# Head loop of a gated-DeltaNet block: the first TensorE level of a triangular inverse by 32x32 corners alone, turned on VectorE

## The chip, the cores and the metric

The kernel runs on one core of one Trainium2 chip. The metric is the device time of one execution in microseconds; the median of several executions is given. All engines of the core (TensorE, VectorE, ScalarE, GpSimd, and SyncE that mostly issues DMAs) have instruction streams of their own and meet at semaphores that the kernel sets and waits for.

## The reference

One decoder block over 1024 tokens of width 1024, in fp32: a mixer (gated DeltaNet beside a short convolution, merged by gates), then a mixture of 32 experts. The part that the change touches is the chunked gated delta rule, with 8 heads of width 128:

```python
    decay = jnp.where(causal, jnp.exp(jnp.where(causal, diff, 0.0)), 0.0)
    k_beta = k * beta
    a = jnp.where(strict, jnp.einsum('bhnik,bhnjk->bhnij', k_beta, k) * decay, 0.0)
    eye = jnp.eye(CHUNK, dtype=a.dtype)
    t_inv = lax.linalg.triangular_solve(eye + a, jnp.broadcast_to(eye, a.shape),
                                        left_side=True, lower=True, unit_diagonal=True)
    u = jnp.einsum('bhnij,bhnjv->bhniv', t_inv, v * beta)
    w = jnp.einsum('bhnij,bhnjk->bhnik', t_inv, k_beta * jnp.exp(g)[..., None])
    intra = jnp.einsum('bhnik,bhnjk->bhnij', q, k) * decay
```

A scan over the chunks follows, which carries a 128x128 state from chunk to chunk. The kernel uses chunks of 128 tokens, so a head has 8 tiles (`TT = 8`), each with a unit lower triangular 128x128 matrix to invert.

## The kernel before

The kernel is one program in stages: adaLN and norm, projections of the short convolution and the gates, the loop over 8 heads, the merge with the output projection, the routing, and the experts. The large projections are fp32 products made of three products of rounded parts (`w_hi`, `w_lo` against `h_hi`, `h_lo`): ScalarE rounds a weight tile to `w_hi` (`split_w_hi`, L698), VectorE subtracts it for `w_lo` (`split_w_lo`, L703), TensorE multiplies (`project`, L769).

In the head loop TensorE's queue is written out by hand, and projections of the same and the next head are put between the small products of the delta rule so that TensorE has work while other engines answer. Part `n` of the third projection of a head (`third(n)`, 2 to 3 of the 8 k-tiles, 6 or 9 products) is such work, and so are the 3-product pieces (`filler`) in the recurrence.

The inverse of each 128x128 triangle grows in levels. VectorE inverts the 16x16 diagonal blocks (`sub_inverse`), results go through DRAM to other lanes (`inverse_rows` on SyncE), GpSimd spreads them over X (L874), VectorE makes the cross blocks that join them to 32x32 (`pair_inverse`), and four DMAs put those into X (L1112, with `base_moved`). X then holds the inverses of the four 32x32 diagonal blocks of each of the 8 tiles. VectorE's transpose (`turn_inverse`, L2103) turns 32x32 blocks, which is a full turn of this block diagonal matrix, and gives Y, the transpose of X.

Two levels on TensorE follow, in `head_pe` and `head_dve`, each over halves `a` of four tiles:

- Level 0 joins 32x32 blocks to 64x64. TensorE multiplies the whole 128x128 `kk_decay` by X (L2905). VectorE scales by -beta and masks with `level_mask` (L2202), which keeps the corner blocks: LX. TensorE multiplies by Y (L2938), VectorE adds the result to X (L2222).
- Level 1 joins 64x64 to 128x128. TensorE multiplies (L2908) and turns X as a whole with eight transposes to PSUM (L2913), from which VectorE copies the new blocks into Y (L2209). VectorE scales (L2197, no mask), TensorE multiplies by Y (L2943), VectorE adds to Y (L2226). X is not needed any more.

Between a level's first and second product TensorE has `third(1)` and `third(2)`, and in front of level 1's second product also eight transposes of v (L2921). VectorE has a weight part (`split_w_lo`) in each level and `q_dec` in the second. Then TensorE makes w from Y (L2950) and the recurrence over the 8 tiles begins (L2980 to L2994), in which the fillers of projection 3 run. Behind it come projection 4, the norm of o, and the keys of the next head. In the last head there is no `third`, and the fillers multiply by `so_hi` and `so_lo`, which DMAs bring back from DRAM (L1151, issued when the head's third projection is done).

The masks are made by GpSimd at the start (L799 to L807). `NL` is the number of levels, `HP` is 64.

Of the kernel before, what the change touches and what calls it, by code (L numbers as in the profile page):

```python
# [5 lines left out]
ALU = mybir.AluOpType  # L6
# [6 lines left out]
P = 128  # L13
# [36 lines left out]
def decoder_block(nc, x, c, w_ada, b_ada, norm1_g, w_in, conv_qkv_w, a_log, dt_bias, onorm_g, w_proj_a,  # L50
# [4 lines left out]
    TT = T // P  # L55
# [17 lines left out]
    LEVELS = [32, 64]  # L73
# [51 lines left out]
    level_mask = at("level_mask", [P, len(LEVELS), P])  # L125
# [314 lines left out]
    with ctx:  # L440
# [332 lines left out]
        def blocks_of(tile, n, odd):  # L773

            return tile.rearrange("p (m s r) -> p m s r", s=2, r=LEVELS[n])[:, :, odd, :]

        def half_dst(bank, t, n):

            return ps[:, bank, (t % 4) * P // 2:(t % 4 + 1) * P // 2].rearrange("p (m r) -> p m r", r=LEVELS[n])

        N_MASKS = 1 + len(LEVELS)

        @block.gpsimd
        def _(pool):
# [5 lines left out]
            pool.memset(level_mask[:], 0.0).then_inc(pool_step, 1)  # L790
            pool.wait_ge(pool_step, 4)
# [6 lines left out]

            for n, b in enumerate(LEVELS):  # L799
                even = level_mask[:, n].rearrange("p (m s r) -> p m s r", s=2, r=b)[:, :, 0, :]  # L800
                src = ones[:].rearrange("p (m s r) -> p m s r", s=2, r=b)[:, :, 0, :]
                m = P // (2 * b)
                pool.affine_select(out=even, in_=src, compare_op=ALU.is_ge, fill=0.0, base=-b,
                                   pattern=[[-2 * b, m], [0, b]], channel_multiplier=1).then_inc(pool_step, 1)
                pool.wait_ge(pool_step, 5 + n)
                pool.affine_select(out=even, in_=even, compare_op=ALU.is_ge, fill=0.0, base=2 * b - 1,
                                   pattern=[[2 * b, m], [0, b]], channel_multiplier=-1).then_inc(masks_done, 1)  # L807

# [4 lines left out]
            pool.wait_ge(pool_step, 6 + len(LEVELS))  # L813
# [85 lines left out]
            pool.wait_ge(pool_step, 9 + len(LEVELS))  # L899
# [836 lines left out]
        def _(dve):  # L1736
# [443 lines left out]
            def head_dve(h, last):  # L2180
# [10 lines left out]

                for n in range(NL):
                    for a in range(2):
                        dve.wait_ge(lx_mm, 2 * NL * h + 2 * n + a + 1)
                        tiles = slice(4 * a, 4 * a + 4)
                        if n == NL - 1:
                            ins = dve.tensor_tensor(  # L2197
                                LX[HP:, tiles, 0:HP], ps[HP:, 6 + a].rearrange("p (t i) -> p t i", i=P)[:, :, 0:HP],
                                hk[HP:, K_NBETA, tiles, None].to_broadcast([HP, 4, HP]), ALU.mult)
                        else:  # L2200
                            for t in range(4 * a, 4 * a + 4):
                                ins = dve.scalar_tensor_tensor(  # L2202
                                    out=LX[:, t], in0=ps[:, 6 + a, (t % 4) * P:(t % 4 + 1) * P],
                                    scalar=hk[:, K_NBETA, t:t + 1], in1=level_mask[:, n], op0=ALU.mult, op1=ALU.mult)
                        ins.then_inc(lx_done, 1)
                        if n > 0:
                            dve.wait_ge(yl_mm, 2 * NL * h + 2 * (n - 1) + a + 1)
                            y_odd = blocks_of(Y[:, tiles].rearrange("p t i -> p (t i)"), n - 1, 1)
                            dve.tensor_copy(y_odd, blocks_of(ps[:, 2 + a], n - 1, 1)).then_inc(y_upd, 1)  # L2209
                    split_w_lo(dve, *(("merge", 0, n) if last else ("head", h, 3 + n)))  # L2210
                    if n == NL - 1:
                        dve.wait_ge(silu_done, 3 * h + 2)
                        dve.wait_ge(grow_in, 16 * h + 32)
                        dve.tensor_tensor(q_dec[:].rearrange("p t i -> p (t i)"), qk[:, 0],
                                          grow[:].rearrange("p t i -> p (t i)"), ALU.mult).then_inc(q_dec_done, 1)
                    for a in range(2):
                        tiles = slice(4 * a, 4 * a + 4)
                        if n < NL - 1:
                            dve.wait_ge(xl_mm, 2 * (NL - 1) * h + 2 * n + a + 1)
                            x_even = blocks_of(X[:, tiles].rearrange("p t i -> p (t i)"), n, 0)  # L2220
                            change = ps[:, 4 + a, 0:2 * P].rearrange("p (m r) -> p m r", r=LEVELS[n])
                            dve.tensor_tensor(x_even, x_even, change, ALU.add).then_inc(x_upd, 1)  # L2222
                        else:
                            dve.wait_ge(yl_mm, 2 * NL * h + 2 * n + a + 1)
                            y_odd = blocks_of(Y[:, tiles].rearrange("p t i -> p (t i)"), n, 1)[0:HP]
                            dve.tensor_tensor(y_odd, y_odd, ps[0:HP, 2 + a, 0:2 * P]  # L2226
                                              .rearrange("p (m r) -> p m r", r=LEVELS[n]), ALU.add).then_inc(y_upd, 1)
# [1050 lines left out]
```

## Time and profile before

| | |
|---|---|
| median of 3 executions | 1977.56 us (1976.2 to 1979.18) |
| the profiled execution, its span | 1977.9 us |
| TensorE busy | 1908.4 us, 96% |
| VectorE busy | 1473.9 us, 75% |
| ScalarE busy | 982.2 us, 50% |
| GpSimd busy | 314.5 us, 16% |
| HBM | 356.89 MB read, 58.06 MB written |

Times in the profile are from the start of the span. An engine row names the line of the kernel that made the instruction. TensorE appears twice: PE for the products, PEld for the weight loads, which run beside them. An fp32 product appears as two records of each; a product of rounded parts and a transpose as one. The start of a record is measured and its end is modelled, so that neighbouring products overlap in the rows and their pace is the distance of their starts.

### The profile page before, as it was taken

The page shows a single profiled execution, that of the slowest core. Times are in us where ns is not written, and L with a number is a line of the kernel's source. Part 1 is how long each engine was busy: PE and PEld are TensorE (multiplying, and loading weights), DVE is VectorE, ACT ScalarE, POOL GpSimd, SP SyncE. Part 2 cuts the span into 40 slices and gives each one's busy share as a digit, 9 for nine tenths or more (in the row PEclk, how much of TensorE's full clock was granted, in tenths as well). Part 3 has the DMA queues.
Part 4 walks back from the last instruction along what each step waited for, and adds up shares of the span by engine and source line. Part 5 has one row for each costly group of instructions (what it writes and reads, how often), then busy time and mean ns, then how long its engine had stood idle before and what let it go on. Part 6 is the DMA issues. An engine that isn't in the chain of part 4 may idle for free.

```text
span 1977.9 us, 28478 instructions
## 1 busy us (share of the span) xinstructions
PE 1908.4 (96%) x9519; PEld 1584.6 (80%) x9519; DVE 1473.9 (75%) x1966; ACT 982.2 (50%) x1354; POOL 314.5 (16%) x243
## 2 busy tenths in 40 slices
PE   5999999999999999999999899998999999999996
PEld 5778888778888888888888787876888888888883
DVE  6966676676756858658577455677999999999996
ACT  5343223301453544535535343125888788788863
POOL 0332323001102101021011000001222222222210
PEclk7999999999999999999999999998999999999998
DMA  8133223687132222222232678437999999999966
GB/s 301 32 82 103 68 80 106 213 294 248 40 106 72 70 75 77 80 70 71 84 93 59 206 266 262 140 143 280 372 383 383 382 380 381 386 387 383 400 252 257
DMA packets 225500, 398.93 MB, mean 202 GB/s; under 512 B 50805, under 2 KB 163878, under 8 KB 199974
## 3 DMA queue, kind: packets, MB, share of 16 engines
q1 hardware_dynamic: 205254, 342.28, 49.8%
q10 hardware_dynamic: 10976, 39.15, 5.1%
q0 software_dynamic: 9216, 16.80, 2.2%
q8 instruction: 32, 0.52, 0.1%
q14 instruction: 22, 0.18, 0.0%
HBM read 356.89 MB, written 58.06 MB: 210 GB/s over the span
## 4 chain that ended last, share of the span: by engine, by line
PE 70%; DVE 13%; DMA 6%; ACT 5%; issue 5%; SPq 1%; ACTq 0%; DVEq 0%; POOL 0%; POOLq 0%
PE ps L3152 17%; PE ps L2756 13%; PE ps L769 12%; PE ps L3196 9%; PE ps L3047 4%; PE ps L2786 3%; PE ps L3138 1%; DVE vv L2019 1%; DMA inv_rows<-inv_d 1%; DMA so_lo<-o_lo_d 1%; DMA inv_d<-sub_x 1%; PE ps L2950 1%; PE ps L2980 1%; PE ps L3176 1%; PE ps L2994 1%
## 5 line engine op out<-in xcount | busy, mean ns | idle before, releaser
L637 DVE TENSOR_TENSOR mw_lo<-mw_raw,mw_hi 128x2048 fp32r<-128x2048 f32 x192 | 436.9, 2290 | 44.0 <-ACT mw_hi L632 43.8
L632 ACT ACTIVATE mw_hi<-mw_raw 128x2048 fp32r<-128x2048 f32 x192 | 368.1, 1919 | 116.2 <-PE ps L3152 67.0
L769 PE MATMUL ps<-h_hi,w_lo 128*128 128x512 f32 x704 | 287.9, 409 | 3.0 <-ACT mod_rows L1447 1.3
L769 PE MATMUL ps<-h_hi,w_hi 128*128 128x512 f32 x704 | 275.5, 391 | 0.0
L769 PE MATMUL ps<-h_lo,w_hi 128*128 128x512 f32 x704 | 274.9, 391 | 0.0
L3152 PE MATMUL ps<-mw_hi,xT_lo 128*128 128x512 f32 x512 | 203.9, 398 | 3.1 <-DVE xT_lo L2525 2.3
L3152 PE MATMUL ps<-mw_hi,xT_hi 128*128 128x512 f32 x512 | 201.1, 393 | 0.0
L3152 PE MATMUL ps<-mw_lo,xT_hi 128*128 128x512 f32 x512 | 200.3, 391 | 0.0
L769 PEld LDWEIGHTS ps<-h_hi,w_hi 128*128 128x128 f32 x704 | 132.6, 188 | 28.4
L769 PEld LDWEIGHTS ps<-h_hi,w_lo 128*128 128x128 f32 x704 | 133.0, 189 | 26.6 <-ACT conv_in L1454 1.8
L769 PEld LDWEIGHTS ps<-h_lo,w_hi 128*128 128x128 f32 x704 | 133.2, 189 | 22.3
L909 POOL DMA_INDIRECT xg<-h_d,tok_now x32 | 80.8, 2524 | 292.8 <-DVE tok_now L2515 276.3
L3152 PEld LDWEIGHTS ps<-mw_hi,xT_lo 128*128 128x128 f32 x512 | 96.8, 189 | 23.3 <-DVE xT_lo L2525 2.9
L3152 PEld LDWEIGHTS ps<-mw_hi,xT_hi 128*128 128x128 f32 x512 | 96.7, 189 | 21.0
L3152 PEld LDWEIGHTS ps<-mw_lo,xT_hi 128*128 128x128 f32 x512 | 96.9, 189 | 19.3
L698 ACT ACTIVATE w_hi<-w_raw 128x1024 fp32r<-128x1024 f32 x60 | 62.1, 1050 | 93.3 <-DMA w_raw<-in_w_proj_b_dram 59.6
L874 POOL TENSOR_TENSOR X<-inv_rows,sub_mask 128x128 f32<-128x128 f32 x64 | 49.2, 804 | 335.2 <-DMA inv_rows<-inv_d 335.2
L1856 DVE TENSOR_TENSOR comb<-ps,comb 128x512 f32<-128x512 f32 x98 | 66.4, 689 | 47.0 <-PE ps L2756 43.9
L3196 PE MATMUL ps<-mw_hi,hidT_lo 128*128 128x512 f32 x248 | 99.2, 400 | 0.0
L703 DVE TENSOR_TENSOR w_lo<-w_raw,w_hi 128x1024 fp32r<-128x1024 f32 x60 | 74.1, 1236 | 30.3 <-ACT w_hi L698 29.0
L3196 PE MATMUL ps<-mw_lo,hidT_hi 128*128 128x512 f32 x248 | 96.7, 390 | 0.0
L3196 PE MATMUL ps<-mw_hi,hidT_hi 128*128 128x512 f32 x248 | 96.6, 390 | 0.0
(436 smaller groups left out, 4042.4 us busy)
## 6 DMA issues: line engine op xcount, KB each, us to landing
mw_raw<-in_w_dram SPq DMA_DIRECT2D x192, 1024.0 KB, 8.2
w_raw<-in_w_in_dram SPq DMA_DIRECT2D x44, 512.0 KB, 5.0
ada_h<-in_w_ada_dram SPq DMA_DIRECT2D x32, 512.0 KB, 6.0
pair_w<-in_w_in_dram SPq DMA_DIRECT2D x28, 512.0 KB, 4.8
y_t<-y_d SPq DMA_DIRECT2D x7, 1024.0 KB, 10.1
ada_sc<-in_w_ada_dram SPq DMA_DIRECT2D x4, 1024.0 KB, 8.7
s_d<-sc_acc ACTq DMA_DIRECT2D x8, 512.0 KB, 5.5
gate_b_d<-gate_sig ACTq DMA_DIRECT2D x8, 512.0 KB, 5.0
```

Of the source, the lines that this page charges most:

```text
L632: act.activation(mw_hi[off % NSPLIT][:], mw_raw[off % NRAW][:], ACT.Copy).then_inc(mw_hi_done, 1)
L637: dve.tensor_tensor(mw_lo[off % NSPLIT][:], mw_raw[off % NRAW][:], mw_hi[off % NSPLIT][:], ALU.subtract).then_inc(mw_lo_done, 1)
L698: act.activation(w_hi[:, t["slot"]], w_raw[:, t["slot"]], ACT.Copy).then_inc(w_hi_done, 1)
L703: dve.tensor_tensor(w_lo[:, t["slot"]], w_raw[:, t["slot"]], w_hi[:, t["slot"]], ALU.subtract).then_inc(w_lo_done, 1)
L769: last = pe.matmul(dst, lhs[:, s, k], rhs[:, k, cols], start=(k == 0 and part == 0), stop=(k == KD - 1 and part == 2))
L909: pool.indirect_dma_start(xg[:, s], None, h2_d, bass.IndirectOffsetOnAxis(tok_now[:, s:s + 1], axis=0), bounds_check=T - 1, oob_is_err=Fal ...
L1856: dve.tensor_tensor(out[:], ps[:, bank], other[:], ALU.add).then_inc(combined, 1)
L2756: last = pe.matmul(ps[:, bank], (op_lo, op_hi, op_hi)[part][o][:, k], moving((0, 1, 0)[part], k), start=(k == 0 and part == 0), stop=(k == ...
L2786: last = pe.matmul(ps[:, 2 + 2 * p + half], (w_lo, w_hi, w_hi)[part][:, s, k], (s_hi, s_lo, s_hi)[part][k][:, cols], start=(k == 0 and par ...
L3047: last = pe.matmul(ps[:, 2 * s + half], lhs, rhs[:, k, half * HALF:(half + 1) * HALF], start=(k == 0 and part == 0), stop=(k == KD - 1 and ...
L3152: last = pe.matmul(dst, lhs[:, k0 + k], rhs[:, cols], start=(first and k == 0 and part == 0), stop=(final and k == 3 and part == 2))
L3196: last = pe.matmul(ps[:, bank + half], lhs[:, 2 * part + f], rhs[:, cols], start=(part == 0 and f == 0 and n == 0), stop=(part == 1 and f ...
```

## The change

The constant `LEVELS = [32, 64]` becomes `BLOCK = 32` and `NL = 2`. `level_mask`, its memset and its four selects on GpSimd go; the numbers of the semaphore waits behind them are lowered.

Level 0 no longer runs over whole 128x128 tiles. It runs over the two corners `g` of the block diagonal (rows of block 2g+1, columns of block 2g) for all eight tiles: 32x32 products into 32 partitions of one PSUM bank per corner, with the corner for t = 0 written with 64 rows (`both_blocks`). VectorE scales one corner of all tiles in one operation, without a mask. The product of the corner with Y gives the corner of X, which VectorE copies instead of adding, and VectorE's transpose turns it into Y. The whole transposes of X on TensorE and the copies from them go. Level 1's first product runs without them and waits for the first corner of X only; the second corner is waited for behind `third(2)`, and Y's corners and level 1's LX in front of the last transpose of v. Level 1's second product uses the lower 64 rows alone, and its result is copied to Y instead of added.

```diff
@@ VectorE, head_dve
-                for n in range(NL):
-                    for a in range(2):
-                        dve.wait_ge(lx_mm, 2 * NL * h + 2 * n + a + 1)
...
-                split_w_lo(dve, *(("merge", 0, n) if last else ("head", h, 3 + n)))
...
+                for g in range(2):
+                    dve.wait_ge(lx_mm, 2 * NL * h + g + 1)
+                    dve.tensor_tensor(LX[odd_block(g), :, even_block(g)],
+                                      corner(6, g).rearrange("p (t i) -> p t i", i=BLOCK),
+                                      hk[odd_block(g), K_NBETA, :, None].to_broadcast([BLOCK, TT, BLOCK]),
+                                      ALU.mult).then_inc(lx_done, 1)
+                split_w_lo(dve, *(("merge", 0, 0) if last else ("head", h, 3)))
+                for g in range(2):
+                    dve.wait_ge(xl_mm, 2 * h + g + 1)
+                    dve.tensor_copy(X[odd_block(g), :, even_block(g)],
+                                    corner(4, g).rearrange("p (t i) -> p t i", i=BLOCK)).then_inc(x_upd, 1)
+                for g in range(2):
+                    dve.wait_ge(x_upd, 2 * h + g + 1)
+                    dve.transpose(Y[even_block(g), :, odd_block(g)], X[odd_block(g), :, even_block(g)]).then_inc(y_upd, 1)
+
+                for a in range(2):
+                    dve.wait_ge(lx_mm, 2 * NL * h + 2 + a + 1)
+                    tiles = slice(4 * a, 4 * a + 4)
+                    dve.tensor_tensor(
+                        LX[HP:, tiles, 0:HP], ps[HP:, 6 + a].rearrange("p (t i) -> p t i", i=P)[:, :, 0:HP],
+                        hk[HP:, K_NBETA, tiles, None].to_broadcast([HP, 4, HP]), ALU.mult).then_inc(lx_done, 1)
+                split_w_lo(dve, *(("merge", 0, 1) if last else ("head", h, 4)))
+                dve.wait_ge(silu_done, 3 * h + 2)
+                dve.wait_ge(grow_in, 16 * h + 32)
+                dve.tensor_tensor(q_dec[:].rearrange("p t i -> p (t i)"), qk[:, 0],
+                                  grow[:].rearrange("p t i -> p (t i)"), ALU.mult).then_inc(q_dec_done, 1)
+                for a in range(2):
+                    tiles = slice(4 * a, 4 * a + 4)
+                    dve.wait_ge(yl_mm, 2 * h + a + 1)
+                    dve.tensor_copy(Y[0:HP, tiles, HP:], ps[0:HP, 2 + a, 0:2 * P].rearrange("p (t i) -> p t i", i=HP))\
+                       .then_inc(y_upd, 1)
@@ TensorE, head_pe
+                pe.wait_ge(base_moved, moved(h, 240))
+                for g in range(2):
+                    for t in range(TT):
+                        rows = odd_block if t else both_blocks
+                        last_mm = pe.matmul(corner(6, g, t, rows), kk_decay[even_block(g), t, rows(g)],
+                                            X[even_block(g), t, even_block(g)], start=True, stop=True)
+                    last_mm.then_inc(lx_mm, 1)
+                if not last:
+                    third(1)
+                pe.wait_ge(kk_done, 4 * h + 4)
+                pe.wait_ge(k_bg_done, TT * h + TT)
+                pe.wait_ge(k_dec_done, TT * h + TT)
+                for g in range(2):
+                    pe.wait_ge(lx_done, 2 * NL * h + g + 1)
+                    pe.wait_ge(base_step, OPS * h + PAIR_OPS + 2)
+                    for t in range(TT):
+                        rows = odd_block if t else both_blocks
+                        last_mm = pe.matmul(corner(4, g, t, rows), Y[odd_block(g), t, rows(g)],
+                                            LX[odd_block(g), t, even_block(g)], start=True, stop=True)
+                    last_mm.then_inc(xl_mm, 1)
+
+                pe.wait_ge(x_upd, 2 * h + 1)
+                for a in range(2):
+                    for t in range(4 * a, 4 * a + 4):
+                        at_ = (t % 4) * P
+                        last_mm = pe.matmul(ps[HP:, 6 + a, at_:at_ + HP], kk_decay[:, t, HP:], X[:, t, 0:HP],
+                                            start=True, stop=True)
+                    last_mm.then_inc(lx_mm, 1)
+                if not last:
+                    third(2)
+                pe.wait_ge(silu_done, 3 * h + 3)
+                pe.wait_ge(x_upd, 2 * h + 2)
+                for t in range(TT):
+                    if t == TT - 1:
+                        pe.wait_ge(y_upd, 2 * NL * h + 2)
+                        pe.wait_ge(lx_done, 2 * NL * h + 4)
+                    last_mm = pe.transpose(ps[:, 4 + t // 4, (t % 4) * P:(t % 4 + 1) * P],
+                                           vv[:, t * P:(t + 1) * P], ident[:])
+                    if t % 4 == 3:
+                        last_mm.then_inc(vt_mm, 1)
+                for a in range(2):
+                    for t in range(4 * a, 4 * a + 4):
+                        last_mm = pe.matmul(ps[0:HP, 2 + a, (t % 4) * HP:(t % 4 + 1) * HP], LX[HP:, t, 0:HP],
+                                            Y[HP:, t, HP:], start=True, stop=True)
+                    last_mm.then_inc(yl_mm, 1)
```

The helpers are `even_block(g)` (rows 64g to 64g+31), `odd_block(g)` (64g+32 to 64g+63), `both_blocks(g)` (64g to 64g+63) and `corner(bank, g, t, rows)`, which is `ps[rows(g), bank + g, 32t:32t+32]`.

## Rows read from the trace of the kernel before

**Rows 1.** The page: busy shares, granted clock in 40 slices, ending chain by engine.
```profile
PE 1908.4 (96%) x9519; PEld 1584.6 (80%) x9519; DVE 1473.9 (75%) x1966; ACT 982.2 (50%) x1354; POOL 314.5 (16%) x243
...
PEclk7999999999999999999999999998999999999998
...
PE 70%; DVE 13%; DMA 6%; ACT 5%; issue 5%; SPq 1%; ACTq 0%; DVEq 0%; POOL 0%; POOLq 0%
```

**Rows 2.** Busy time by stretch: from:to, length, busy PE PEld DVE ACT POOL, clock.
```profile
613.00:693.00 80.00, 79.66 (x456) 67.78 (x455) 55.75 (x108) 37.07 (x81) 10.46 (x10) 1.00 0.27 77
...
614.83:623.32 8.49, 8.18 (x67) 7.07 (x65) 7.70 (x18) 3.44 (x4) 0.00 (x0) 1.00 0.00 0
```

**Rows 3.** Chain of waits, 600 to 700 us: start, duration, engine and line.
```profile
600.88 2.64 DMA inv_rows<-inv_d
...
617.54 0.92 DVE LX L2202 x4
...
623.56 2.08 PE ps L769 x9
...
627.62 2.05 PE ps L2950 x16
...
648.56 0.71 PE ps L769 x3
...
697.36 1.00 DVE LX L2202 x4
```

**Rows 4.** Timeline of the second head: start, duration, engine, line, operation, tiles, count.
```profile
611.39 1.74 SPq L1112 DMA_DIRECT2D X<-cross_d  x4
...
614.83 1.95 PE L2905 MATMUL ps<-X,kk_decay 128*128 128x128 f32 x16
...
616.25 1.30 DVE L2103 STREAM_TRANSPOSE Y<-X 128x512 f32<-128x512 f32 x2
...
618.44 0.39 PE L769 MATMUL ps<-h_hi,w_hi 128*128 128x512 f32 x1
618.98 1.97 PE L2938 MATMUL ps<-LX,Y 128*128 128x64 f32 x16 [0.15 <-issue]
...
619.50 1.22 DVE L703 TENSOR_TENSOR w_lo<-w_raw,w_hi 128x1024 fp32r<-128x1024 f32 x1
620.63 0.77 DVE L2222 TENSOR_TENSOR X<-X,ps 128x256 f32<-128x256 f32 x2
621.10 0.68 PE L2908 MATMUL ps<-X,kk_decay 128*64 128x64 f32 x8 [0.15 <-DVE X L2222]
621.71 0.66 PE L2913 MATMUL ps<-ident,X 128*128 128x128 f32 x4
...
623.32 0.47 PE L769 MATMUL ps<-h_hi,w_lo 128*128 128x512 f32 x1
...
625.48 1.03 PE L2921 MATMUL ps<-ident,vv 128*128 128x128 f32 x8
```

**Rows 5.** Weight loads by line: durations ns min/median/max, first and last start us.
```profile
L2905 PEld LDWEIGHTS ps<-X,kk_decay x128: 187/192/193, 535.3 to 1099.9; 128*128 128x128 f32 x128
...
L2684 PEld LDWEIGHTS ps<-h_lo,w_gate_parts x16: 107/108/108, 80.0 to 92.3; 128*32 128x32 f32 x16
...
L2692 PEld LDWEIGHTS ps<-fold,gate_rows x16: 181/187/187, 98.5 to 100.2; 32*128 32x128 f32 x16
```

**Rows 6.** The view of tile X: its DMAs from issue to landing.
```profile
DMA to landing us min/median/max: 1.5/1.7/1.9
```

**Rows 7.** Timeline at the start of the span and in the first head.
```profile
9.93 3.51 PE L2660 MATMUL ps<-ident,x_n 128*128 128x128 f32 x16 [9.93 <-DVE x_n L1769]
...
546.49 1.01 PEld L2943 LDWEIGHTS ps<-Y,LX 128*64 128x64 f32 x16 [0.17 <-issue]
```

**Rows 8.** Timeline of the last head: first DMA for so_hi, and TensorE's wait for them.
```profile
1098.50 0.35 SPq L1151 DMA_DIRECT2D so_hi<-o_hi_d  x1
...
1112.25 0.50 PE L769 MATMUL ps<-so_hi,w_lo 128*128 128x512 f32 x1 [1.08 <-DMA so_lo<-o_lo_d]
```

More of the change, by code:

```diff
@@ L72, in decoder_block @@
     PAIR = 2 * SUB
-    LEVELS = [32, 64]
+    BLOCK = 32
+    NL = 2
     NSUB = P // SUB
@@ L124, in decoder_block @@
     later = at("later", [P, P])
-    level_mask = at("level_mask", [P, len(LEVELS), P])
     sub_mask = at("sub_mask", [P, P])
@@ L771, in project, with even_block, odd_block, both_blocks @@
             return last
[L773 to L781, printed above, removed]
+        def even_block(g):
+            return slice(2 * g * BLOCK, (2 * g + 1) * BLOCK)
+        def odd_block(g):
+            return slice((2 * g + 1) * BLOCK, (2 * g + 2) * BLOCK)
+        def both_blocks(g):
+            return slice(2 * g * BLOCK, (2 * g + 2) * BLOCK)
+        def corner(bank, g, t=None, rows=odd_block):
+            cols = slice(0, TT * BLOCK) if t is None else slice(t * BLOCK, (t + 1) * BLOCK)
+            return ps[rows(g), bank + g, cols]
+        N_MASKS = 1
         @block.gpsimd
@@ L789, in _ @@
             pool.memset(eps_col[:], EPS).then_inc(pool_step, 1)
-            pool.memset(level_mask[:], 0.0).then_inc(pool_step, 1)
-            pool.wait_ge(pool_step, 4)
+            pool.wait_ge(pool_step, 3)
             pool.affine_select(out=ident[:], in_=ident[:], compare_op=ALU.not_equal, fill=1.0, base=0,
@@ L797, in _ @@
                                pattern=[[-1, P]], channel_multiplier=1).then_inc(masks_done, 1)
[L799 to L807, printed above, removed]
             pool.affine_select(out=sub_mask[:].rearrange("p (m r) -> p m r", r=SUB), in_=ones[:].rearrange(
@@ L812, in _ @@
             pool.memset(sub_eye[:], 0.0).then_inc(pool_step, 1)
-            pool.wait_ge(pool_step, 6 + len(LEVELS))
+            pool.wait_ge(pool_step, 5)
             pool.affine_select(out=sub_mask[:].rearrange("p (m r) -> p m r", r=SUB), in_=sub_mask[:].rearrange(
@@ L898, in _ @@
             pool.memset(xg[:], 0.0).then_inc(pool_step, 1)
-            pool.wait_ge(pool_step, 9 + len(LEVELS))
+            pool.wait_ge(pool_step, 8)
             for n in range(2):
@@ L2190, in head_dve @@
                 turn_inverse(h)
-                for n in range(NL):
-                    for a in range(2):
-                        dve.wait_ge(lx_mm, 2 * NL * h + 2 * n + a + 1)
[L2195 to L2209, printed above, removed]
-                    split_w_lo(dve, *(("merge", 0, n) if last else ("head", h, 3 + n)))
[L2211 to L2227, printed above, removed]
@@ L2270, in head_dve @@
                 dve.tensor_tensor(o_lo[:], o_raw[:], o_hi[:], ALU.subtract).then_inc(o_hi_done, 1)
-            NL = len(LEVELS)
             with dve.Fori(0, H - 1) as h:
@@ L2303, in _ @@
             dve.wait_ge(params_in, 16 * 10)
-            dve.wait_ge(pool_step, 8 + len(LEVELS))
+            dve.wait_ge(pool_step, 7)
             steps = [0]
@@ L2821, in _ @@
             pe.wait_ge(gb_sig, past(2 * KD))
-            NL = len(LEVELS)
             o_squares = LX[:].rearrange("p t i -> p (t i)")
```

48 lines of the change are left out of this document (removed).

## The prediction

> **What bounds the kernel now.** I read the page first. TensorE is busy for 96% of the span at a granted clock that stays at its upper level (2.4 GHz) almost everywhere, and 70% of the chain that ended last is TensorE's [rows 1]. The change touches the inverse in the loop over the eight heads (its first products start between 535 and 1100 us [rows 5]) and a few masks built at the very start, so the next view is the busy time by stretch. A steady head takes 80.0 us, and TensorE is busy for 79.66 of them; the first level of the inverse alone, from its first product to the end of its part of the second, takes 8.49 us [rows 2]. So in this loop an engine-microsecond of TensorE is a microsecond of the kernel, unless something else takes over.
>
> The chain of waits shows how close that something is. It does not stay on TensorE: from the end of the recurrence (648.56) it goes over ScalarE's evacuation and VectorE to the small inverses, their DMAs (600.88 is that place one head earlier), VectorE's pair products, its value convolution, the turn of X and the LX products (617.54, and 697.36 one head on), and only behind those back to TensorE [rows 3]. The two LX rows are 79.82 us apart. TensorE's own queue and this VectorE/DMA chain are therefore nearly equally long; both run through the stretch from 617.5 to 627.6 that the change rewrites, so a saving there shortens both. That is the reason to count it in full, head after head.
>
> In the timeline of that stretch [rows 4] the reader is to see three things. First, the 16 records of L2905 (8 products; each fp32 product is two records) start 0.112 us apart ((1.95 - 0.275)/15), and so do those of L2938 although they stream only 64 columns: they are paced by their 128 weight columns. Second, TensorE waits twice for VectorE: L2938 could start at 618.67 (618.44 + 0.23) and starts at 618.98; L2908 starts at 621.10, right behind the first X addition (620.63 + 0.42), and with the change of shape told next it could at 620.94. Together about 0.45 us. Third, a change of tile shape costs (L2908 works on 64 columns, the transposes L2913 on 128). L2908's last record starts at 621.10 + 0.68 - 0.22 = 621.56, the first transpose behind it at 621.71, 0.15 later and not 0.06; the four transposes then need (0.66 - 0.27)/3 = 0.129 and not 0.109 each, the pace of the eight transposes of v ((1.03 - 0.27)/7). Together 0.15 us a change.
>
> **What is removed, per head.** TensorE: 16 records of L2905 at 0.112 = 1.79 us; 16 of L2938 at 0.112 = 1.79; 8 transposes of X (L2913) at 0.109 = 0.87; and the four changes of shape that L2908 and L2913 make in turn, 0.60. Sum 5.05. VectorE: eight LX products, two X additions (0.77 us) and two Y copies.
>
> **What is added, per head.** TensorE: 2 x 8 corner products for LX and 2 x 8 for X, 64 records, with 32 weight columns, 32 moving columns and 32 rows (64 weight columns for t = 0). Call one record's spacing s. Changes of shape: into the corners, t = 0 to t = 1, corner 0 to corner 1, t = 0 to t = 1 again, and out, five for LX and five for X, and one from L2908 back to the projection: 11 x 0.15 = 1.65. Net on TensorE: 5.05 - 1.65 = 3.40 us less, 64 s more.
>
> No row has a record with 32 weight columns and few moving ones, so s is bounded. From above by the 64-column record: the 16 weight loads of L2943 are (1.01 - 0.14)/15 = 0.058 apart [rows 7]. From below by the line through 128 columns (0.112) and 64 (0.058), which gives 0.032 at 32 (an estimate; the single load shortens on such a line too, 192 ns at 128 columns and 108 at 32 [rows 5]). Thirty-two rows alone change nothing: L2692 has them, and its 16 loads run from 98.5 to 100.2, again 0.112 apart [rows 5]. I take s = 0.040, nearer to the line, since the measured loads shorten with the columns all the way, but above it, since a fixed cost per record would show first at the smallest size. Then TensorE's own work falls by 3.40 - 2.56 = 0.84 us a head (1.35 at 0.032; -0.31, longer, at 0.058).
>
> **The stretch played through for head 1, with s = 0.040.** TensorE starts at 614.83 as before; LX corners take 1.28 + 0.60, to 616.71; the nine projection products (2.04 at their pace of 0.23, as in the x9 of [rows 3], and one change) end at 618.90. VectorE still ends its turn of X at 617.55 and makes two LX corners (256 elements a lane as in L2222, 0.42 each) by 618.4, the weight part L703 by 619.6. So TensorE has no wait, does the X corners to 620.78 and is ready for L2908 at 620.93. The first X copy needs the first corner's products (619.8, and 0.2 for their end, the length of a product in L2908) and is there at 620.5. L2908 (16 x 0.058) ends at 621.86, and the projection starts at 622.0 where it started at 623.32: 1.3 us earlier. Behind it VectorE has the second copy (621.4), two transposes of 256 elements (0.42 each, to 622.25), two LX products for level 2, L703 and q_dec (1.22 each, for the same 1024 elements a lane): done at 625.6. TensorE reaches L2943 at 625.14, its first half is out at 625.8, the Y copy follows, and L2950 starts at 626.3 for 627.62. The gain is 1.3 us a head: 0.84 of work and 0.45 of waits. The bounds of s give 1.7 to 1.8 and 0.05 to 0.15.
>
> **Other edits, and what covers them.** TensorE's transposes of v now wait in front of the last one for Y's transposes and for level 2's LX (623.1 here); that one is due at about 624.9, and behind it only L2943 is queued, which needs both anyway. The wait for the second X copy (621.4) stands behind the projection's third part and is 2 us early. ScalarE's copies of v follow the earlier transposes and were idle before them. X must have landed when the corners start: the last of four DMAs is issued by 613.13 and lands 1.7 us later, 614.8 for a start at 614.83 [rows 4, 6]. There is no room in front of the stretch, but that landing is in the chain behind the recurrence and moves with it. The masks: GpSimd drops one memset and four selects at the head of the span, while TensorE's first product starts at 9.93 and had waited for VectorE's x_n [rows 7]: nothing.
>
> **The sum.** In the last head nothing is gained: behind L2980 TensorE waits for the DMAs of so_hi and so_lo until 1112.25, and those are issued from 1098.50, as soon as the projection in front of the corners is done [rows 8]; a shorter inverse makes that wait longer. Seven heads remain: 7 x 1.3 = 9.1 us. The profiled execution has a span of 1977.9 us, 0.3 above the median of the runs shown, 1977.56, so the sum can be set against either: 1977.6 - 9.1 = 1968.5.
>
> **Rivals.**
> 1. *A floor per record.* If a record costs 0.058 however small it is, 64 records and the changes of shape eat what the removed ones gave: -0.31 of work against 0.45 of waits, 0.1 us a head, and 1977 in all. For it: twice the columns take 0.112 and not 0.116, so a record has a fixed part, and no smaller one shows whether that grows into a floor. Chance 0.20.
> 2. *Slower: small tiles don't hide their weight loads.* If in a 32x32 tile the next load can't run under the product in front of it, a record costs its load, 0.108 and more; at the 0.112 of L2905, 64 s is 7.17, TensorE's work grows by 3.77 a head, less 0.45 of waits: 3.3 x 7 = 23, and 2 more in the last head past its DMA wait: 2003. It decides from s = 0.060 on (3.85/64). Against it: in L2943 loads start 0.058 apart, each itself 0.14 long, so that neighbours overlap each other and the products between them [rows 7]. Chance 0.13. The Trainium skill (TensorE: Matmul & The Clock Gate, section on packing small matmuls) says that a weight load overlaps a running matmul only when its row group differs. Here all eight products of a corner have one row group, so by that rule a record would cost a whole load and a whole product, 0.108 and about 0.2, and the kernel some 120 us more; the loads of L2943 overlap on equal rows, which the rule excludes, so I give this form 0.03 of the 0.13.
> 3. *VectorE takes over.* The new chain runs LX corners, L703, X copy, with 0.4 us of room at L2908 and 0.2 at the Y copy. If each of the eight operations on other partitions than the one before starts 0.1 later, L2950 slips by 0.4 to 0.6 and the gain is 0.8 a head: 1972. Chance 0.12. The Trainium skill (VectorE: DVE Perf Modes, section on two Vector instructions with no wait between them) says that an operation whose output starts in another quadrant starts only when all earlier ones have finished; the two X additions here, in one quadrant, overlap by 0.07 (0.77 for 2 x 0.42), and by the rule the new ones would not, 0.4 us on VectorE.
> 4. *The time comes back at the next head.* If X's landing does not move with the recurrence, L2905's place waits for what was saved: 1977. The chain [rows 3] speaks against it. Chance 0.05.
>
> **How the numbers follow.** The forecast, s between 0.032 and 0.05, has 0.50 and ends at 1968.5. Faster by over 0.2% (4 us; about what a measurement of this kernel can tell from no change) are the forecast and rival 3: 0.62. Within 0.2% are rivals 1 and 4: 0.25. Slower is rival 2: 0.13. The range goes down to 1961 (s = 0.032 and the changes from t = 0 to t = 1 free, 0.6 a head more: 7 x 2.35 = 16.5) and up to 1980.5, which takes in rivals 1, 3 and 4 and leaves rival 2 out.
>
> **What would show it.** In the profile of the changed kernel: 64 corner records a head, 0.03 to 0.05 apart, with gaps of 0.15 at the changes; L2908 starting 6.1 us behind the corners' first product, where it is 6.27 now; the projection behind it 7.2 behind, now 8.49; a head period of 78.7 us, now 80.0. Spacings of 0.058 or more, a wait of L2908 for the X copy, or a wait for X's DMA that grows by what was saved would each make the prediction wrong, for rivals 1 or 2, 3 and 4.

## The result and the profile after

| | before | after |
|---|---|---|
| median of the executions | 1977.56 us | 1965.72 us |
| lowest and highest | 1976.2 to 1979.88 | 1964.42 to 1968.72 |
| span of the profiled execution | 1977.9 us | 1962.5 us |

The ratio is 0.9942 (95% interval 0.993 to 0.9954): the change makes the kernel 11.8 us faster, 0.6%. On another chip, beside two of the experiments below (e6_late and e7_order), the same two kernels gave 1978.62 and 1966.66 us, ratio 0.9936 (0.992 to 0.9951). Forecast were 1968.5 us and a range of 1961 to 1980.5.

The page of the changed kernel: busy time, granted clock, and the chain that ended last.

```profile
PE 1897.8 (97%) x9711; PEld 1573.4 (80%) x9711; DVE 1465.7 (75%) x1918; ACT 982.6 (50%) x1354; POOL 313.7 (16%) x238
...
PEclk7999999999999999999999899988999999999998
...
PE 84%; DVE 5%; DMA 5%; ACT 2%; issue 2%; SPq 1%; ACTq 0%; POOL 0%; DVEq 0%; POOLq 0%
```

TensorE has 192 records more and is busy for 10.6 us less. In the chain that ended last its share rose from 70 to 84% and VectorE's fell from 13 to 5% [rows 1]: in the steady heads the detour over VectorE and the DMAs [rows 3] is gone from the chain.

**Where the time went.** Busy time by stretch, from the first product of level 0 in head 0 to that of head 7, in the kernel before and then in the changed one (columns as in [rows 2]):

```profile
535.49:1098.31 562.82, 561.02 (x3198) 477.58 (x3197) 390.62 (x751) 260.78 (x569) 73.16 (x70) 1.00 0.27 76
```
```profile
532.01:1082.56 550.55, 550.25 (x3365) 464.69 (x3365) 383.11 (x709) 260.65 (x569) 73.16 (x70) 1.00 0.27 78
```

Seven head periods shrank by 12.27 us, 1.75 each. The busy columns split this into 10.77 us less work on TensorE and 1.50 us less waiting, of which 0.30 is left; since a product's end is modelled, part of every wait stands in them as busy time, and the starts of the products, used further below, give 2.9 us of waits. From head 7's first product to the end of the span it is 1977.9 - 1098.31 = 879.6 us before and 1962.5 - 1082.56 = 879.9 after. So the gain lies in the seven heads. (That last stretch is from 878.0 to 883.7 us long in the ten profiled executions of this document, so equality to 0.3 us is chance.)

The two spans differ by 15.4 us, 3.5 more than the medians allow. That part lies ahead of head 0 and is TensorE's clock. Busy time by stretch of before, then of after:

```profile
402.00:406.00 4.00, 3.81 (x10) 3.00 (x11) 3.82 (x6) 0.00 (x0) 0.00 (x0) 0.57 1.00 322
...
477.00:481.00 4.00, 4.00 (x12) 3.10 (x11) 3.81 (x6) 0.00 (x0) 0.00 (x0) 0.57 0.98 282
```
```profile
402.00:406.00 4.00, 4.00 (x19) 3.29 (x18) 3.82 (x6) 0.00 (x0) 0.00 (x0) 1.00 1.07 353
...
477.00:481.00 4.00, 4.00 (x19) 3.32 (x18) 3.90 (x9) 0.60 (x1) 0.21 (x1) 1.00 0.38 133
...
1092.00:1096.00 4.00, 4.00 (x20) 3.89 (x18) 0.42 (x1) 0.67 (x2) 0.00 (x0) 0.50 1.03 421
```

Before ran mostly at 1.2 GHz in these two stretches (and in one at 112 us), ten and twelve products where after has nineteen; after had such a stretch in the last head instead. In the first of them TensorE had waited 1.47 us for VectorE's `w_lo` just ahead, in both kernels, and the clock fell in one of the two. The profiled execution of the changed kernel when it ran again had other places once more and the same seven heads (550.56 us). Over the ten profiled executions the start of head 0 goes roughly with the number of such stretches between 100 us and it: 532.01 us with none, 532.69 and 533.25 with one, 533.55 to 535.86 with two, and 535.49 with the three of before. So this part is not put down to the change, and heads are compared from here on, not spans.

**The stretch of head 1**, chain of waits of after, which here is TensorE alone:

```profile
610.15 1.56 PE ps L2886 x32
611.71 2.29 PE ps L769 x9
614.00 1.56 PE ps L2899 x32
615.56 1.07 PE ps L2907 x16
616.63 2.28 PE ps L769 x9
618.91 0.87 PE ps L2918 x8
619.79 1.07 PE ps L2924 x16
620.86 0.04 issue
620.90 2.05 PE ps L2931 x16
...
688.24 1.56 PE ps L2886 x32
```

L2886 and L2899 are the corner products (L2905 and L2938 before), L2907 and L2924 level 1's two products (L2908, L2943), L2918 the transposes of v (L2921), L2931 makes w (L2950). The head period is 688.24 - 610.15 = 78.09 us, for 80.0.

VectorE beside it, timeline of the same head:

```profile
611.42 1.30 DVE L2097 STREAM_TRANSPOSE Y<-X 128x512 f32<-128x512 f32 x2
612.74 0.88 DVE L2188 TENSOR_TENSOR LX<-ps,hk 32x256 f32<-32x256 f32 x2
613.65 1.23 DVE L703 TENSOR_TENSOR w_lo<-w_raw,w_hi 128x1024 fp32r<-128x1024 f32 x1
614.91 0.42 DVE L2195 COPY X<-ps 32x256 f32<-32x256 f32 x1
615.59 0.43 DVE L2195 COPY X<-ps 32x256 f32<-32x256 f32 x1 [0.27 <-PE ps L2899]
```

The first X copy ends at 615.33 and L2907, which needs it, starts at 615.49 in TensorE's timeline. Where it does wait for this copy (e3_few below) it starts 0.05 us behind the copy's end. That is a near tie: 0.1 us of room, where the forecast had 0.4.

### The profile page after: what moved, and what is told of

Same layout as the page of the kernel before. It is cut to its first block, busy times and chain, and to the rows that moved or that the text cites. A ratio compares the mean times of both kernels' runs of the same rounds, so it can differ in the third digit from the quotient of the medians.

```text
span 1962.5 us, 28802 instructions
## 1 busy us (share of the span) xinstructions
PE 1897.8 (97%) x9711; PEld 1573.4 (80%) x9711; DVE 1465.7 (75%) x1918; ACT 982.6 (50%) x1354; POOL 313.7 (16%) x238
## 4 chain that ended last, share of the span: by engine, by line
PE 84%; DVE 5%; DMA 5%; ACT 2%; issue 2%; SPq 1%; ACTq 0%; POOL 0%; DVEq 0%; POOLq 0%
PE ps L769 24%; PE ps L3133 17%; PE ps L2744 13%; PE ps L3177 9%; PE ps L3028 4%; PE ps L2774 3%; PE ps L3119 1%; DMA so_lo<-o_lo_d 1%; PE ps L2961 1%; PE ps L2931 1%; PE ps L2836 1%; PE ps L2865 1%; PE ps L2975 1%; PE ps L3157 1%; PE ps L2964 1%
```

## The experiments

The theories: **P** (the prediction's): both parts of the change shorten TensorE's queue, the removed transposes of X with their changes of shape by about 1.2 us a head, the corners by the rest, each record (one of the two entries that an fp32 product makes in the trace) costing what its weight columns cost. **V**: the queue is already so short that VectorE's chain (LX corners, weight part, X copy) sets the head, so that making TensorE shorter still gives little. **D**: 32x32 tiles in different rows and columns of the array run side by side, so that the order of the corners matters. The first four kernels ran beside 17 executions of the kernel before (median 1979.04 us), the next three beside 11 (1978.62), the last beside 9 (1978.36). The ratio compares a kernel with its own neighbours; medians of different chips are not to be compared with each other. "Seven heads" is always the time from head 0's first product of level 0 to head 7's, in one profiled execution.

| | median us | ratio (95%) | seven heads | TensorE busy in them |
|---|---|---|---|---|
| before | 1977.56 | | 562.82 | 561.02 |
| e1_turn | 1970.11 | 0.9953 (0.994 to 0.9966) | 555.16 | 553.42 |
| changed kernel | 1965.72 | 0.9942 (0.993 to 0.9954) | 550.55 | 550.25 |
| e2_wide | 1970.84 | 0.9951 (0.9938 to 0.9964) | 553.20 | 552.91 |
| e3_few | 1964.24 | 0.9928 (0.9916 to 0.9941) | 549.11 | 545.85 |
| e4_vload | 1975.11 | 0.9981 (0.9972 to 0.999) | 559.46 | 553.77 |
| e6_late | 1963.02 | 0.9921 (0.9908 to 0.9933) | 547.10 | 545.76 |
| e7_order | 1967.34 | 0.994 (0.9927 to 0.9952) | 549.81 | 541.84 |
| e8_best | 1961.98 | 0.992 (0.9906 to 0.9934) | 548.37 | 541.93 |

**The turn alone (e1_turn).** The kernel before, with its whole products and masks, but Y's new blocks come from VectorE's transpose; the PE transposes of X and the Y copies are gone.

```diff
-                        if n > 0:
-                            for t in range(4 * a, 4 * a + 4):
-                                last_mm = pe.transpose(ps[:, 2 + a, (t % 4) * P:(t % 4 + 1) * P], X[:, t], ident[:])
-                            last_mm.then_inc(yl_mm, 1)
...
+                            if a == 1:
+                                dve.wait_ge(x_upd, 2 * h + 2)
+                                for g in range(2):
+                                    even, odd = slice(64 * g, 64 * g + 32), slice(64 * g + 32, 64 * g + 64)
+                                    dve.transpose(Y[even, :, odd], X[odd, :, even]).then_inc(y_upd, 1)
```

> The kernel before with one part of the change alone: VectorE turns the two corners of X into Y, and the eight whole transposes of X on TensorE with their two copies go. The whole-tile products, the masks and the adds stay. Theory P (TensorE's own work in the stretch sets the time): eight transposes at 0.109 us and two of the four changes of tile shape (0.15 each) go, 1.1 to 1.2 us a head in seven heads, 8 us: 1969.5, two thirds of the whole gain. Rival C (the corners bring most of it, because the products shrink from 128 to 32 columns): only the eight transposes' overlap goes, 3 us: 1974.5.

Measured: 562.82 - 555.16 = 7.66 us in seven heads, 1.1 each, as P expected. So about five eighths of the change's 12.27 us come from taking the transposes of X off TensorE, and three eighths (4.61 us, 0.66 a head) from the corners. By the busy columns the corners' share is 3.17 us of TensorE work and 1.44 us of waits.

**64 weight columns in every corner record (e2_wide).**

```diff
-                        rows = odd_block if t else both_blocks
+                        rows = both_blocks
```

> The changed kernel with 64 weight columns in all corner products and not for t = 0 alone: 56 records a head grow from 32 to 64 weight columns, and the four changes of tile shape between t = 0 and t = 1 go. Theory P: a record costs its weight columns (0.032 us at 32, 0.058 at 64), so +1.47 us, less 4 x 0.12 for the changes, +1.0 a head: seven heads, 1972.7. Rival F (a record has a cost that does not depend on its columns, the changed kernel is bound by something else): 1965.7, or 1962 if only the changes of shape count.

Measured: 2.65 us more in seven heads, 0.38 each, not 1.0. The source views of L2886, of the changed kernel and of e2_wide, and e2_wide's chain:

```profile
L2886 PEld LDWEIGHTS ps<-X,kk_decay x256: 101/108/132, 532.0 to 1084.0; 32*32 32x32 f32 x112, 32*64 32x64 f32 x16
```
```profile
L2886 PEld LDWEIGHTS ps<-X,kk_decay x256: 127/133/133, 534.7 to 1089.5; 32*64 32x64 f32 x128
```
```profile
613.17 1.77 PE ps L2886 x32
...
617.20 1.77 PE ps L2899 x32
```

A corner stage (both corners of one product) grew from 1.56 to 1.77 us. Within a corner the records start 0.058 apart, as priced, but 32 of them would be 1.86 and not 1.77: corner 1's first record starts 0.006 us behind corner 0's thirteenth, and the two run side by side, as D has it. The expectation had taken off the four changes of shape between t = 0 and t = 1, but not the two more between corner 0 and corner 1, which here have one shape, and not that overlap. The direction of P stands (cost follows the columns), its size for this edit does not.

**Wide for the first record only (e3_few).** 64 columns in corner 0's t = 0 alone; the 32-column form elsewhere, and both LX corners waited for together.

```diff
-                        rows = odd_block if t else both_blocks
+                        rows = odd_block if t or g else both_blocks
...
+                pe.wait_ge(lx_done, 2 * NL * h + 2)
+                pe.wait_ge(base_step, OPS * h + PAIR_OPS + 2)
                 for g in range(2):
-                    pe.wait_ge(lx_done, 2 * NL * h + g + 1)
-                    pe.wait_ge(base_step, OPS * h + PAIR_OPS + 2)
```

> The changed kernel with 64 weight columns only for the first product of a level (corner 0, t = 0), so that two pairs of wide records and four changes of tile shape a head go; the second corner's product waits together with the first. Theory P: 0.27 us less in each of the two corner groups, 0.54 a head, 3.8 in seven heads: 1962. Theory V (VectorE's chain of turn, LX corners, weight part and first X copy is only 0.1 us shorter than TensorE's queue at the level's end): TensorE waits for the X copy at level 1's first product, 0.1 a head, 1965.

TensorE's work fell by 550.25 - 545.85 = 4.40 us, the seven heads by 1.44. The rest became idle time: 549.11 - 545.85 = 3.26 us, where the changed kernel has 0.30. Waits of TensorE between 610 and 1010 us (total us, times, longest), the product in head 1's timeline, and VectorE ahead of it:

```profile
PE ps L2907 <- DVE X L2195: 2.3, 6, 0.4
```
```profile
617.16 1.15 PE L2907 MATMUL ps<-X,kk_decay 128*64 128x64 f32 x16 [0.38 <-DVE X L2195]
```
```profile
615.43 1.23 DVE L703 TENSOR_TENSOR w_lo<-w_raw,w_hi 128x1024 fp32r<-128x1024 f32 x1
616.69 0.88 DVE L2195 COPY X<-ps 32x256 f32<-32x256 f32 x2
```

The X copy starts as soon as VectorE's weight part is done (616.66), so VectorE's own queue is what TensorE waits for. (A smaller part of the idle time, about 0.1 us a head in front of L2899, comes with the edit itself, which makes corner 0 wait for LX of both corners.) V is right from here on: the changed kernel stands close to the point where the two chains are equally long.

**VectorE made later (e4_vload).** One more VectorE operation of 1.22 us between the weight part and the X copies.

```diff
                 split_w_lo(dve, *(("merge", 0, 0) if last else ("head", h, 3)))
+                dve.tensor_tensor(q_dec[:], kk_decay[:], kk_decay[:], ALU.mult)
                 for g in range(2):
```

> The changed kernel with one more VectorE operation of 1024 elements a lane (1.22 us; its result is written over by the right one later) between the weight part and the X copies. Theory V: level 1's first product starts later by 1.22 less 0.1 of room, +1.1 a head, seven heads: 1973.4, with a wait of TensorE of 1.1 us in front of it. Rival S (VectorE has room, since its total work is only 55 of 78 us a head): 1965.7, no new wait.

```profile
PE ps L2908 <- DVE X L2196: 4.5, 5, 1.2
```
```profile
618.00:620.40 2.40, 1.52 (x30) 1.41 (x29) 2.29 (x5) 0.00 (x0) 0.00 (x0) 1.00 0.00 0
620.40:623.80 3.40, 3.40 (x11) 2.66 (x10) 3.34 (x5) 0.00 (x0) 0.00 (x0) 0.53 0.00 0
```

Undisturbed heads behind the first take 78.9 to 79.0 us, 0.9 more, and level 1's first product starts 6.36 us behind the corners instead of 5.41. So 0.9 of the 1.22 us of VectorE work is paid, where V expected 1.1. Two of the seven heads took 80.6 and 80.9: behind a wait of 0.88 us for the X copy the granted clock was 0.53 (mostly 1.2 GHz) from 620.4 to 623.8, and again in the sixth head, which adds 1.6 and 1.9 us to them. Four other heads waited 0.76 to 0.89 us at the same place and kept the upper level, so the wait alone does not decide it.

**VectorE made earlier (e6_late).** e3_few, with both weight parts moved behind the Y copies.

```diff
-                split_w_lo(dve, *(("merge", 0, 0) if last else ("head", h, 3)))
...
-                split_w_lo(dve, *(("merge", 0, 1) if last else ("head", h, 4)))
...
                        .then_inc(y_upd, 1)
+                for n in range(2):
+                    split_w_lo(dve, *(("merge", 0, n) if last else ("head", h, 3 + n)))
```

> The kernel of e3_few (wide records only for the first product of a level), with both weight parts of VectorE moved behind the Y copies, so that its X copies follow the products directly. Theory V (in e3_few the heads are 77.95 us long where TensorE's own queue would give the 77.49 of its first head, because level 1's first product waits for the X copy): the copy is there 0.3 us earlier, heads of 77.6, 2 us less than e3_few, 1.5 to 3 more than that if VectorE was late elsewhere too. Rival W (the weight parts, now 5 us later, delay the next head's weight DMAs or the recurrence's first state): heads longer than 77.95.

The work on TensorE stays (545.76), its idle time falls from 3.26 to 1.34 us, and the seven heads come down by 2.01 us against e3_few (later heads 77.5 to 77.7, as V expected). Together with e4_vload this brackets V: the same engine, moved either way, moves the head.

**The changed kernel again (e5_after).**

> The changed kernel once more, beside the others of this call. Expected: the ratio of the first measurement, 0.994, and heads of 78.07 us; the place and the number of the stretches with the halved clock, and with them 1 to 3 us of the span, may differ from execution to execution.

It gave 1966.66 us, ratio 0.9936, seven heads 550.56 us.

**The corners in turn (e7_order).** The loops exchanged, so that neighbouring records belong to different corners. The X product's loops are exchanged in the same way, and it waits for LX of both corners.

```diff
-                for g in range(2):
-                    for t in range(TT):
+                for t in range(TT):
+                    for g in range(2):
...
-                    last_mm.then_inc(lx_mm, 1)
+                        if t == TT - 1:
+                            last_mm.then_inc(lx_mm, 1)
```

> The changed kernel with the two corners of a level in turn (t outside, corner inside) and not one after the other. In the trace of e2_wide the second corner's first four products ran under the first corner's last ones, 0.006 us apart, although nothing there asks for it. Theory D (products in different row and column groups run side by side): the 32 records of a level take about 0.9 us from the first start to the last and not 1.5. Rival Q (weight loads still go one after the other, 0.032 each): 1.3 us, only the changes of tile shape gone. In both cases the head gets at most 0.15 us shorter, 78.07 to 77.95, since VectorE's X copy then is what level 1 waits for (theory V): ratio 0.9935. Without V, 76.8 us and 0.990.

Weight loads of L2886 in head 1, the changed kernel first, then e7_order, and e7_order's waits:

```profile
610.08 1.52 PEld L2886 LDWEIGHTS ps<-X,kk_decay 32*64 32x64 f32 x32 [0.35 <-issue]
```
```profile
612.93 0.75 PEld L2886 LDWEIGHTS ps<-X,kk_decay 32*64 32x64 f32 x32 [0.35 <-issue]
```
```profile
PE ps L2909 <- DVE X L2195: 4.6, 6, 0.8
PE ps L2900 <- DVE LX L2188: 2.6, 6, 0.7
```

D is right: the same 32 records start within 0.64 us (0.75 less one load of 0.108) instead of 1.41. TensorE's busy time falls by 8.41 us, although a halved-clock stretch in the third head (79.46 us where its neighbours take 77.8) adds 1.7 to it:

```profile
696.00:701.00 5.00, 4.97 (x27) 4.22 (x28) 4.45 (x7) 0.00 (x0) 0.00 (x0) 0.66 0.03 5
```

Its idle time in the seven heads rises from 0.30 to 549.81 - 541.84 = 7.97 us, the waits above, so that the seven heads fall by 0.74 only (2.4 without the halved clock, 0.3 a head; V had said at most 0.15). The median (1967.34) is not below the changed kernel's on the same chip (1966.66): corner 0 now ends with corner 1, VectorE gets both late, and TensorE waits for LX and for the X copy: V again.

**Both (e8_best).** Corners in turn, and both weight parts behind the Y copies.

> The two edits that each gained, together: the first level's corners in turn (t outer, g inner) and both VectorE weight parts behind the Y copies. Corners in turn alone left TensorE's queue so short (32 records in 0.67 us instead of 1.47) that its heads of 77.8 us waited for VectorE (4.6 us in six heads for the X copy, 2.6 for LX); the late weight parts alone left heads of 77.6. If VectorE's chain from LX to the X copy holds the head (V), taking 0.4 us of weight work out of it lets the head fall to TensorE's own queue, 77.0 to 77.1 us as the first head of the run with corners in turn shows it (77.08): 7 x 0.5 = 3.5 us below the run with late weight parts, about 1959.5 us, ratio 0.9905. If what remains of the chain (LX copies, first X copy) is as late as before without the weight part (N), heads stay at 77.5 to 77.6, the time at about 1963 and the ratio at 0.992, with TensorE's wait for the X copy at 0.4 to 0.6 us in each head.

```profile
PE ps L2909 <- DVE X L2194: 3.0, 6, 0.5
PE ps L2900 <- DVE LX L2188: 2.6, 6, 0.6
```
```profile
607.08 0.76 DVE vv L2013
...
612.08 1.30 DVE Y L2097 x2
...
613.41 0.42 DVE LX L2188
...
613.86 0.44 DVE LX L2188
...
614.42 0.91 PE ps L2900 x32
615.34 0.41 DVE X L2194
...
615.79 1.15 PE ps L2909 x16
```

It measured as N says: 1961.98 us, ratio 0.992, head 0 at 77.10 us and the undisturbed later ones at 77.5 to 77.7, no better than e6_late's 77.5 to 77.7 (one head with a halved-clock stretch took 79.3 and is why its seven heads are the longer sum). What V expected was wrong in one point: the weight part was not the only VectorE work in front. The second view, the chain of waits in head 1, comes from the value convolution (L2013) over the turn of X and both LX corners, with TensorE only as a step between them. That chain is what stands in the way below 77.5 us a head; none of these edits shortens it, so that it is the limit is read from the trace and was not tried. e8_best has the fastest median, 16.4 us below that of before beside it; the intervals of its ratio and e6_late's overlap, and which of the two is better is not settled. e6_late is 3.6 us below the changed kernel on the same chip (1966.66); its seven heads are 3.46 shorter, while the intervals of the two ratios just overlap.

## Why the prediction was right, point by point

**The bound.** Right: TensorE work removed inside the head loop came off the time head for head, and the VectorE/DMA chain [rows 3] did not hold it up. It moved along, and it was near: 0.1 us at L2907. e1_turn shows this without the corners: 7.60 us less work on TensorE, seven heads 7.66 shorter.

**What a record costs.** Taken 0.040 us between two records of 32 columns, bounds 0.032 and 0.058: too high by a quarter. Two clusters of TensorE's timeline in the changed kernel give it; the first holds records 1 to 5 of corner 0, the second records 2 to 16:

```profile
610.08 0.50 PE L2886 MATMUL ps<-X,kk_decay 32*64 32x32 f32 x5
```
```profile
610.16 0.77 PE L2886 MATMUL ps<-X,kk_decay 32*64 32x32 f32 x15
```

With 0.191 for one record, the fifth starts at 610.39 and the sixteenth at 610.74: 0.35/11 = 0.032 us each. The lower bound, the straight line through 128 and 64 columns, is the price; the 0.008 that I had added for a fixed cost is not there. Rivals 1 and 2 fall with it. So does the rule of the Trainium skill that stood beside rival 2 (TensorE: Matmul & The Clock Gate, packing small matmuls): on one row group, loads of 0.108 us start 0.032 apart, each overlapping the three before it. The measurement decides.

**What a change of shape costs.** Taken 0.15. A corner takes 1.56/2 = 0.78 us: fourteen records at 0.032 and two of 64 columns at 0.058 make 0.56, and the 0.22 left are two changes, 0.11 each. The Trainium skill (TensorEngine Tiling (Array Packing), Key Properties) says that a change of the tiling mode drains TensorE; the trace agrees that it costs, 0.11 us here and 0.15 at L2908 before.

**The stage and the stretch.** A corner stage was forecast at 1.28 + 0.60 = 1.88 us and took 1.56. The 0.32 are 28 x 0.008 = 0.23 of pace and 4 x 0.04 = 0.16 of changes, less 4 x 0.018 = 0.07 for the four wide records, which the sum had priced as narrow. This term, twice in each head, is the one that was mis-sized:

| us behind the first corner product | forecast | measured |
|---|---|---|
| level 1's first product | 6.1 | 5.41 |
| projection behind it | 7.2 | 6.5 |
| w (L2950, now L2931) | 11.5 | 10.82 |
| head period | 78.7 | 78.09 |

**The gain per head.** Forecast 1.3 for all seven, 0.84 of work and 0.45 of waits; measured 1.26 in head 0 and 1.7 to 1.95 in the others, 12.27 in all for 9.1. Head 0 had no waits to lose. Its products of before, up to level 1's first, follow each other at once, where in head 1 L2938 starts 0.54 behind the last projection product and L2908 0.43 behind L2938's last record [rows 4]:

```profile
539.11 0.40 PE L769 MATMUL ps<-h_hi,w_hi 128*128 128x512 f32 x1
539.34 1.90 PE L2938 MATMUL ps<-LX,Y 128*128 128x64 f32 x16
541.17 0.68 PE L2908 MATMUL ps<-X,kk_decay 128*64 128x64 f32 x8
```

Here the distances are 0.23 and 0.21. So the 1.26 us of head 0 are work alone, for 0.84: the two corner stages gave 0.64 more than forecast, and other terms took about 0.2 back (L2905's records, for one, held TensorE for 1.71 us up to the next projection product and not for 1.79). That head 0 came out at 1.3 is luck: 0.42 too little work and 0.45 of waits that were not there cancel. In heads 1 to 6 the same distances give 0.37 to 0.58 us of waits, 2.9 in all, and the reading of 0.45 a head was right there. The profile's idle time shows only 1.50, because it begins at a product's modelled end. With 0.032 for a record the forecast's own sum would have been 1.8 a head, 12.6 in all.

**The base of the sum.** The step that set the span of 1977.9 beside the median was loose. The changed kernel's profiled execution took 1964.6 us with a span of 1962.5, so 2.1 us lie around the span; by that, the execution profiled before stood about 2.4 us above its median, and it has three stretches at a halved clock ahead of head 0 that the other does not have. The forecast 1968.5 is the median less 9.1, so no number changes.

**The last head.** Right. TensorE's timeline of the changed kernel:

```profile
1082.56 1.63 PE L2886 MATMUL ps<-X,kk_decay 32*64 32x32 f32 x32
...
1096.41 0.50 PE L769 MATMUL ps<-so_hi,w_lo 128*128 128x512 f32 x1 [0.18 <-DMA so_lo<-o_lo_d]
```

The product that needs `so_lo` comes 13.85 us behind the first corner product, and it came 13.94 behind it before (1112.25 [rows 8] less 1098.31): the DMA sets its place. How the time saved ahead of it is passed differs. In this execution most of it went into a halved clock (0.50 in the stretch from 1092 to 1096 above), and the wait for `so_lo` was 0.18 us, against 1.08 before. In e5_after's execution, with a shorter such stretch, the distance was 13.70 and the wait 0.90 us:

```profile
1097.51 0.50 PE L769 MATMUL ps<-so_hi,w_lo 128*128 128x512 f32 x1 [0.90 <-DMA so_lo<-o_lo_d]
```

All nine profiled executions other than before's, e1_turn's included, have a halved-clock stretch in the last head, and before's has none. Whether the change brings it was not tried; a loss of one or two us by it would not show in the scatter of 878.0 to 883.7 us. **The masks.** Right as far as the traces show: e1_turn still builds them and starts head 0 at 532.69 us, between the two executions of the changed kernel (532.01 and 533.25).

**Rival 3 (VectorE takes over).** It did not decide, but its chance was set too low. The room was 0.1 and not 0.4 us, because VectorE kept its forecast times up to the weight part (LX corners done 3.5 us behind the first product, weight part 4.8): its first X copy was done 0.4 us earlier than forecast (5.25 behind the first product for 5.67) and TensorE came 0.7 earlier. Its step was of the right size: two LX corners in different quadrants take 0.88 us, two X additions in one took 0.77 [rows 4], 0.4 in all for the eight operations. That is what the rule of the Trainium skill (VectorE: DVE Perf Modes, two Vector instructions with no wait between them) had given, and the trace agrees with it. e3_few shows what follows as soon as TensorE gains another 0.6 us a head: 4.40 us of work saved, 1.44 us of time.

**Rival 4 (the time comes back at the next head).** Excluded: seven heads, seven gains, and the changed kernel's steady heads lie within 0.04 us of each other.

## What to carry to other kernels

Price small fp32 products that follow each other in one place of the array by their weight columns alone, down to 32, and put the changes of tile shape into the sum as a cost of their own, about 0.11 to 0.15 us each: eight transposes of 128 columns with their changes were worth more here than 64 records of 32 columns in place of 32 records of 128. When an edit shortens the bounding engine's queue, compute the room of each answer from the other engines again with the *new* queue times; here 0.7 us more speed than forecast turned 0.4 us of room into 0.1, and further savings on TensorE were worth a third of themselves (e3_few) or less (e7_order). Compare a loop period between the same two marks, not two spans, when the clock's stretches differ between executions.

## What was not expected of the hardware

- 32x32 products in different rows and columns of the array run side by side: in turn, 32 fp32 records start within 0.64 us, two by two 0.007 us apart, for 1.41 us corner by corner. The same page of the Trainium skill (TensorEngine Tiling (Array Packing), Key Properties) says that tiles load and multiply in parallel, and the trace agrees.
- Fp32 weight loads on one row group overlap several deep: 0.108 us long, 0.032 apart.
- TensorE's clock fell to its lower level in a steady head only in kernels where TensorE waited 0.5 us or more there (e4_vload twice, e7_order and e8_best once in seven heads; never in those of the changed kernel, e1_turn, e2_wide, e3_few or e6_late). That is 4 heads of the 21 of these three kernels; most of the 21 had such waits too and kept the upper level. That a wait causes it was not tried by itself.
